# Last layer's expert rows: from indirect DMAs to products with one-hot matrices

## The reference

```
cap = EC_CAPACITY * n // N_EXPERTS                      # 2 * 512 / 16 = 64 rows per expert
affinity = softmax(h @ router_w + router_b)             # h: (512, 1024)
gates, idx = top_k(affinity.T, cap)                     # 16 experts, each picks its 64 tokens
xg = h[idx]                                             # 64 rows for each expert
hid = silu(xg @ w_gate) * (xg @ w_up)                   # weights 1024 x 1024
y = (hid @ w_down) * gates
out = zeros((512, 1024)).at[idx].add(y)                 # a token may be chosen by several experts
```

## Time and profile before

| | us |
|---|---|
| median of 3 runs (lowest, highest) | 2129.21 (2127.64, 2328.96) |
| the profiled execution's own time | 2131.61 |
| its span, first to last instruction | 2129.7 |
| PE busy | 1938.7 (91%) |
| DVE busy | 634.7 (30%) |
| ACT busy | 504.4 (24%) |
| POOL busy | 215.2 (10%) |
| mean granted TensorE clock | 0.966 of full speed |

### The profile page before, as it was taken

The page is one execution under the profiler, slowest core; times in us unless marked ns, Lnnn a source line. Parts: engine busy times, 40 slices in busy tenths (PEclk is TensorE's granted clock), DMA queues, the critical chain, the costliest instruction groups (busy, mean ns, idle before and its releaser), DMA issues. The chain is left out here.

```text
span 2129.7 us, 25643 instructions
## 1 busy us (share of the span) xinstructions
PE 1938.7 (91%) x10794; PEld 952.4 (45%) x10794; DVE 634.7 (30%) x1198; ACT 504.4 (24%) x999; POOL 215.2 (10%) x235
## 2 busy tenths in 40 slices
PE   5998999989999999999998989999898988778777
PEld 2656465544433333333334856655445323323222
DVE  2357552372431111111114366523523000000002
ACT  4145541542200000000004155514321000000002
POOL 1400000120011121211101000001101100000010
PEclk9999999999999999999998999999999998988998
DMA  9620304121389999999999123024419999999997
GB/s 348 181 79 4 136 1 165 73 79 40 113 337 399 396 394 401 393 399 396 393 389 357 45 80 139 1 81 157 158 68 403 398 401 405 401 401 405 401 401 301
DMA packets 168003, 538.73 MB, mean 253 GB/s; under 512 B 11273, under 2 KB 19795, under 8 KB 167891
## 3 DMA queue, kind: packets, MB, share of 16 engines
q1 hardware_dynamic: 149232, 489.49, 58.9%
q0 software_dynamic: 17856, 45.46, 7.2%
q10 hardware_dynamic: 802, 2.16, 0.3%
HBM read 510.08 MB, written 27.00 MB: 252 GB/s over the span
## 5 line engine op out<-in xcount | busy, mean ns | idle before, releaser
L2982 PE MATMUL ps<-ring,arena 128*64 128x512 f32 x1024 | 238.2, 616 | 25.1 <-DMA ring<-in_w_up 10.3
L2982 PE MATMUL ps<-arena 128*64 128x512 f32 x768 | 190.8, 646 | 33.2 <-DMA arena<-in_w_up 16.4
L2269 PE MATMUL ps<-arena,ring 128*128 128x256 f32 (+1 forms) x640 | 191.4, 460 | 2.4 <-DMA ring<-in_w_in 2.4
L2982 PEld LDWEIGHTS ps<-ring,arena 128*64 128x64 f32 x1024 | 76.3, 141 | 173.8 <-issue 172.5
L2269 PEld LDWEIGHTS ps<-arena,ring 128*128 128x128 f32 x640 | 120.9, 190 | 73.5 <-issue 61.1
L2175 DVE TENSOR_TENSOR arena<-arena,ps 128x512 f32<-128x512 f32 x32 | 22.0, 688 | 425.9 <-ACT arena L1414 425.9
L2822 PE MATMUL ps<-ring,arena 128*128 128x512 f32 x320 | 144.0, 605 | 0.6 <-ACT arena L1369 0.6
L2982 PEld LDWEIGHTS ps<-arena 128*64 128x64 f32 x768 | 61.8, 148 | 151.5 <-issue 151.5
L1414 ACT ACTIVATE arena<-ps 128x512 f32<-128x512 f32 x32 | 19.1, 597 | 447.6 <-PE ps L2982 447.6
L3019 PE MATMUL ps<-arena 128*64 128x512 f32 x488 | 109.7, 594 | 1.4 <-ACT arena L1437 1.4
L3019 PE MATMUL ps<-ring,arena 128*64 128x512 f32 x448 | 101.5, 595 | 3.1 <-DMA ring<-in_w_down 3.1
(11 more groups left out here) (382 smaller groups left out, 2572.7 us busy)
## 6 DMA issues: line engine op xcount, KB each, us to landing
ring<-in_w_gate SPq DMA_DIRECT2D x32, 2048.0 KB, 20.9
ring<-in_w_up SPq DMA_DIRECT2D x32, 2048.0 KB, 15.9
ring<-in_w_down SPq DMA_DIRECT2D x28, 2048.0 KB, 22.8
ring<-in_ada_w SPq DMA_DIRECT2D x24, 2048.0 KB, 11.1
arena<-in_w_down SPq DMA_DIRECT2D x22, 2048.0 KB, 23.1
arena<-in_w_gate SPq DMA_DIRECT2D x17, 2048.0 KB, 23.4
arena<-in_w_up SPq DMA_DIRECT2D x17, 2048.0 KB, 21.1
ring<-in_w_in SPq DMA_DIRECT2D x6, 2048.0 KB, 13.2
```

The costliest lines, as they stand in the source:

```text
L2269: ins = mm(o[0:n, c0:c1], w[:, k, col:col + n], hT[:, k, c0:c1], start=k == 0, stop=k == KD - 1)
L2982: ins = mm(px[0][hf * 64:hf * 64 + 64, col:col + 512], xl[e % 2][:, at:at + CAP_L], w[c][:, hf * 512:hf * 512 + 512], start=b + c == 0, st ...
```

## The change

Only the last layer changes. The homes "a" and "c" are dropped, so weights have nine homes, and "d" (the eleventh before) is the ninth. `htok` stays in SBUF, and `Fa` holds the sums there. The rows are no longer stored, gathered, added in HBM or loaded back. POOL issues nothing for the experts but one load of the table `last_no` (it tells for each column which token it is), early in the layer.

In their place, for each expert x:

- `picks(x)` (DVE, two instructions of 64 partitions by 256) compares `last_no` with the expert's row numbers and gives a one-hot matrix; `picks_turned(x)` (PE) turns it with two transposes, `picks_out(x)` (ACT) copies it from PSUM.
- `rows_up(x)` (PE) makes 8 products of the turned picks with `htok`, `picked_out(x)` (ACT) copies the rows from PSUM, and `latent_rows_turned` goes on from there.
- `spots(e)` (DVE, four instructions of 128 by 128) gives four one-hot matrices, one for each tile of 128 tokens.
- `sums_up(e, p0, p1)` (PE) makes the pieces p0 to p1 of eight, one for each tile and half of the columns. A piece is one product with 64 rows. The pieces take two PSUM banks in turn, and a piece waits until the piece two before it has been taken out.
- `sums_added(e)` (DVE) takes each piece out: for expert 0 with a copy, for the others with an addition to `Fa`, 128 by 512.

```diff
-LAST_HOMES = [0, 1, "dead", "wide", 2, 3, "b", "x", "c", "a", "d"]
+LAST_HOMES = [0, 1, "dead", "wide", 2, 3, "b", "x", "d"]
...
ACT:
                 for e in range(NE):
+                    more = not ctx_on and e + 2 < NE
                     if not ctx_on and e == NE - 1:
                         weighted(e - 1)
+                    if more and e:
+                        picks_out(e + 2)
                     hidden(e)
+                    if more:
+                        if e == 0:
+                            picks_out(2)
+                        picked_out(e + 2)
...
DVE:
+                def picks(x):
+                    dve.wait_ge(s_no, 16)
+                    if x:
+                        dve.wait_ge(S["picks_turned"], x)
+                    for h in range(2):
+                        r = slice(h * CAP_L, (h + 1) * CAP_L)
+                        ins = dve.tensor_scalar(pick[r, :], last_no[r, h * 256:(h + 1) * 256], last_rows[r, x:x + 1], None,
+                                                ALU.is_equal)
+                    ins.then_inc(S["picks_ready"], 1)
...
+                def sums_added(e):
+                    for n in range(2 * (NT - CT) * e, 2 * (NT - CT) * (e + 1)):
+                        src, _, t, hf = sum_piece(px, n)
+                        dst = Fa[:, CT + t, hf * 512:(hf + 1) * 512]
+                        dve.wait_ge(S["sums_full"], n + 1)
+                        if e:
+                            dve.wait_ge(S["sums_out"], n + 1 - 2 * (NT - CT))
+                            TT(dst, dst, src, ALU.add).then_inc(S["sums_out"], 1)
+                        else:
+                            dve.tensor_copy(dst, src).then_inc(S["sums_out"], 1)
...
                     if not ctx_on and e == NE - 1:
+                        sums_added(NE - 3)
+                        spots(NE - 1)
+                        sums_added(NE - 2)
...
+                    if not ctx_on and 2 <= e < NE - 1:
+                        sums_added(e - 2)
+                        spots(e)
                     if e + 2 < NE:
                         modulated_lat(e + 2)
                         if ctx_on:
                             modulated_ctx(e + 2)
+                        elif e + 3 < NE:
+                            picks(e + 3)
...
PE:
+                def picks_turned(x):
+                    pe.wait_ge(S["picks_ready"], x + 1)
+                    if x:
+                        pe.wait_ge(S["rows_out"], x)
+                    for c in range(2):
+                        ins = pe.transpose(px[3][:, 512 + c * P:512 + (c + 1) * P], pick[:, c * P:(c + 1) * P], ident)
+                    ins.then_inc(S["picks_turned"], 1)
+                def rows_up(x):
+                    pe.wait_ge(S["picks_out"], x + 1)
+                    for t in range(NT - CT):
+                        h, c = divmod(t, 2)
+                        for hf in range(2):
+                            ins = mm(px[3][hf * CAP_L:(hf + 1) * CAP_L, 512:1024],
+                                     pick_turned[:, c * P + h * CAP_L:c * P + (h + 1) * CAP_L],
+                                     htok[:, t, hf * 512:(hf + 1) * 512], start=t == 0, stop=t == NT - CT - 1)
+                    ins.then_inc(S["rows_up"], 1)
+                def sums_up(e, p0, p1):
+                    if p0 == 0:
+                        pe.wait_ge(S["y_lat"], n0 + e + 1)
+                        pe.wait_ge(S["spots_ready"], e + 1)
+                    for n in range(2 * (NT - CT) * e + p0, 2 * (NT - CT) * e + p1):
+                        o, i, t, hf = sum_piece(px, n)
+                        half = slice(hf * CAP_L, (hf + 1) * CAP_L)
+                        if n >= 2:
+                            pe.wait_ge(S["sums_out"], n - 1)
+                        mm(o, spot_tiles[i % 2][t][half, :], y_l[i % 2][half, :], start=True, stop=True)\
+                            .then_inc(S["sums_full"], 1)
...
                     ins = lat(0, gate, 0)
                     if e == 0:
                         ins.then_inc(S["gate_used"], 1)
+                        if not ctx_on:
+                            rows_up(1)
...
                     ins.then_inc(S["blocks_used"], 1)
+                    if not ctx_on and e == NE - 1:
+                        sums_up(NE - 2, 0, 8)
...
                 def down(e, n):
+                    sums = not ctx_on and 1 <= e < NE - 2
+                    if sums:
+                        sums_up(e - 1, 0, 3)
...
                     ins.then_inc(S["blocks_used"], 1)
+                    if sums:
+                        sums_up(e - 1, 3, 6)
...
                     latent_down(1, w).then_inc(S["down_lat"], 1)
+                    if sums:
+                        sums_up(e - 1, 6, 8)
...
-                busy_meanwhile(6 if ctx_on else 16)
+                if ctx_on:
+                    busy_meanwhile(6)
+                else:
+                    picks_turned(0)
+                    busy_meanwhile(4)
+                    rows_up(0)
+                    busy_meanwhile(4)
...
                 for e in range(NE):
+                    more = not ctx_on and e + 2 < NE
+                    if not ctx_on and e == NE - 1:
+                        sums_up(NE - 3, 0, 8)
+                    if more and e:
+                        picks_turned(e + 2)
                     gate_up(e, BLOCKS[l].index((0, e, 0)))
+                    if more and e:
+                        rows_up(e + 2)
+                    elif more:
+                        picks_turned(2)
...
                     hidden_turned(e)
+                    if more and e == 0:
+                        rows_up(2)
```

More of the change, by code:

```diff
@@ L392, in block_homes @@
         return [n % XRING[l] for n in range(6 * NE)]
-    return [LAST_HOMES[n % XRING[l]] for n in range(6 * NE - 1)] + ["d"]
+    return [LAST_HOMES[n % XRING[l]] for n in range(6 * NE)]
 def earlier_blocks(l, n):
@@ L640, in build @@
         rows_hbm = nc.dram_tensor("normed_rows", (TOK, D), F32).ap()
-        sum_hbm = [nc.dram_tensor(f"expert_sums{l}", (TOK, D), F32).ap() for l in range(DEPTH)]
+        sum_hbm = [nc.dram_tensor(f"expert_sums{l}", (TOK, D), F32).ap() for l in range(DEPTH - 1)]
         x_hbm = nc.dram_tensor("residual", (TOK, D), F32).ap()
@@ L890, in _ @@
                     pool.wait_ge(s_zero, 4)
-                    for l1 in range(DEPTH):
+                    for l1 in range(DEPTH - 1):
                         for t in query_tiles(l1):
@@ L935, in _ @@
                     pool.dma_start(Xt(t), src).then_inc(x_back[t], 16)
+                if l == DEPTH - 1:
+                    load(last_no, T["const"][:, K_END:K_END + SEQ], s_no)
                 for i, t in enumerate(q):
@@ L1419, in weighted, with picks_out, picked_out @@
                     if e >= 2:
-                        act.wait_ge(put_lat, 16 * (n0 + e - 1))
+                        act.wait_ge(*((put_lat, 16 * (n0 + e - 1)) if ctx_on else (S["sums_full"], 2 * (NT - CT) * (e - 1))))
                     act.activation(y_l[e % 2], px[1][:, 512:1024], ACT.Copy, scale=row_gate[:, e:e + 1]).then_inc(S["y_lat"], 1)
[L1423 to L1426, removed]
+                def picks_out(x):
+                    act.wait_ge(S["picks_turned"], x + 1)
+                    if x:
+                        act.wait_ge(S["rows_up"], x)
+                    act.activation(pick_turned, px[3][:, 512:768], ACT.Copy).then_inc(S["picks_out"], 1)
+                def picked_out(x):
+                    act.wait_ge(S["rows_up"], x + 1)
+                    if x:
+                        act.wait_ge(S["lat_turned"], n0 + x)
+                    act.activation(picked, px[3][:, 512:1024], ACT.Copy).then_inc(S["rows_out"], 1)
+                if not ctx_on:
+                    for x in range(2):
+                        picks_out(x)
+                        picked_out(x)
                 for e in range(NE):
+                    more = not ctx_on and e + 2 < NE
                     if not ctx_on and e == NE - 1:
                         weighted(e - 1)
+                    if more and e:
+                        picks_out(e + 2)
                     hidden(e)
+                    if more:
+                        if e == 0:
+                            picks_out(2)
+                        picked_out(e + 2)
                     if e == NE - 1:
@@ L2130, in _ @@
                 dve.wait_ge(*v.next(dve_step))
-                if not ctx_on:
-                    dve.tensor_copy(last_row, rows[:, 2 * NE - 1:2 * NE])
-                dve.tensor_copy(row_no[:, 0:NE], rows[:, NE:2 * NE])
+                if ctx_on:
+                    dve.tensor_copy(row_no[:, 0:NE], rows[:, NE:2 * NE])
+                else:
+                    dve.tensor_copy(last_rows, rows[:, NE:2 * NE]).then_inc(dve_step, 1)
+                    dve.wait_ge(*v.next(dve_step))
                 phase()
@@ L2155, in _ @@
                     modulated_ctx(1)
+                if not ctx_on:
+                    picks(0)
```

(12 more changed lines are left out.)

75 lines of the change are left out of this document (40 added, 35 removed).

## The result

The changed kernel takes 2231.96 us (median of 4 runs, 2227.15 to 2234.04). It is slower by 4.8%: the ratio to the kernel before is 1.0477, 95% interval 1.0456 to 1.0499. The forecast was 2211 us, 3.8% slower. The profiled execution took 2232.13 us, its span is 2230.3. One run of the kernel before, the 2328.96 us in the table, was in a slow state of the chip, and the ratio leaves it out.

A forecast was written before the change was run, and what follows sets the result against it. DMA was taken to bound the kernel before (32.7 us an expert), PE after (35.9). The start to 1690.6, experts 2 to 15 to 2181.6 and an end of 29.4 give a span of 2211.0; forecast 2211 us, range 2148 to 2240.

The forecast's parts named there:

- PE becomes the bound: Last layer's experts: PE needs 35.9 us for each, above the 30.7 that DMA needs, so PE sets the pace.
- The wait for the picks: Ahead of gate-and-up PE waits 3.0 us for DVE's picks (bounds 1.9 and 3.8), 2.2 in experts 0 and 1.
- The clock: Behind each picks wait gate-and-up starts at a low clock: 1.7 us more (bounds 0 and 3.4).
- The sums: Eight sum pieces for each expert on PE, in bursts of three, three and two: 5.7 us.
- The start: First products at 1631, table load behind gate_up(0), gate_up(1) at 1661.2, gate_up(2) at 1690.6 us.
- Rival A: PE keeps up and DMA stays the bound, an expert under 30.7 us: 2111 us, 0.8% faster; chance 0.12.
- Rival B: PE is the bound, but the picks wait is hidden and the clock stays up: 31.2 us an expert, 2149; chance 0.08.
- Rival C: Short gaps in the sum bursts, three per expert, keep the clock low for much of down: 2263 us; chance 0.06.

The follow-up runs named there:

- e6: The changed kernel with one home fewer ("d" dropped, eight left): 2230.46 us, ratio 1.0465.
- e1: The changed kernel with DVE making picks(e+3) right behind the hidden rows of expert e, ahead of taking out the sums: 2171.16 us, ratio 1.0200.
- e2: The changed kernel with six filler products on PE in front of each picks_turned: 2215.54 us, ratio 1.0409.
- e3: The changed kernel with the eight sum pieces as four pairs in place of three, three and two: 2211.57 us, ratio 1.0371.
- e4: The changed kernel with both the earlier picks and the sums in pairs: 2134.92 us, ratio 1.0032.
- e7: e4 with the sums of experts 12, 13 and 14 all in pairs in the last two experts: 2131.73 us, ratio 1.0001.
- e11: e7 with an earlier diagonal, last sum pair moved into the last up products, fewer fillers around rows_up(0), seven more ahead of the picks: 2125.45 us, ratio 0.9984.

## Why the prediction was right, and where it was off

- **PE becomes the bound.** Right, in mechanism and path. DMA falls to 336 GB/s in the eleven experts (about 350 forecast), the waits for weights are gone, and e6 shows that homes don't matter.
- **The wait for the picks.** Forecast 3.0 us for each expert and 2.2 twice at first; measured 3.08 and 2.13. DVE's list was as counted: its two picks take 0.71 us in place of 0.55, the spots 0.8. e1 shows that it was on the path in full.
- **The clock.** Forecast 1.7 us behind each wait, measured 1.65 by e2. e3 shows that it isn't a constant: 4.80 to 6.16 us for the same 16 records behind the same wait.
- **The sums.** This is the term that was mis-sized. I put a burst of three at 2.3 us, within bounds of 1.6 and 2.6; it measured 2.95, above the upper one. Two things were wrong. I let the first piece end 0.8 us into the burst, but DVE begins with it only 1.16 us behind the burst's start (1895.93 against 1894.77), as late as it does behind the lone third piece (1897.83 against 1896.67). And I gave the third piece 0.7 us, but alone it takes 1.05, as long as a pair. Both together are 0.65 us for a burst, 1.3 for an expert. Down beside them took 7.2 us for 6.9, rows_up 3.5 for 3.4: 16 records take 3.43 us from start to start between groups of their own shape, and 3.53 to 3.59 next to one of another shape. So 37.65 in place of 35.9. From gate_up(2) to gate_up(13), eleven experts, this made 19.6 us, in experts 13 and 14 another 1.4, and in expert 15 1.7, where a burst of eight took 7.4 us and not 6.6.
- **The start.** gate_up(2) began 3.3 us earlier than forecast. I had kept the table load of 1.28 us behind gate_up(0). It ran at 1638.1, right behind ACT's copy of the picked rows, and was out of the way; why it ran ahead there and not before isn't shown. rows_up(2) took 3.65 us for 4.5, the first gate product came 0.6 earlier, and expert 1 took 0.4 less. (The terms that the prediction gives from gate_up(0) to gate_up(1) add up to 1660.6 and not to its 1661.2.)
- **The sum of these:** 2211.0 - 3.3 + 19.6 + 1.4 + 1.7 = 2230.4, the span is 2230.3. That the start was put too late hid a part of what the sums were put too low; this much was luck. The measured 2232 lies near the upper end of the range, 2240.
- **Rival A** (DMA stays the bound, 2111 us) needed an expert in under 30.7 us. e4 shows that this could be had with another order. It then comes to 2135, not to 2111. Part of the difference is PE work outside the steady loop, the last experts' sums and the first rows: e7 to e11 took 10 us out of it. The rest no run takes apart.
- **Rival B** (no picks wait, clock up) didn't come true in the changed kernel, but e1 is what it describes. Its 31.2 us came out as 32.7, by the same mis-sized sums and neighbours.
- **Rival C** (the short gaps between pieces pull the clock down). An expert has two such gaps, one in each burst of three, and not the three that the prediction counts. In the bursts of two and three the clock didn't fall: e1 has all these gaps and a clock of 1.00 in its windows. In the bursts of eight at the end it did in 5 of 14. I had set the rival aside by an idle stretch of 1.48 us between dense products; these bursts suggest that such a stretch says little on groups of 64-row products, but no run tests that by itself. The Trainium skill, "TensorE: Matmul & The Clock Gate", section "A second HAM failure mode: psum-queue depth-cycling", tells of a kernel in which small idle gaps between groups of products that cycle through PSUM banks let the clock swing. The traces here agree in part: in e2's second burst of eight the clock fell to 0.76 (2170 to 2184 us) with only such gaps in it, while the same gaps left the changed kernel's clock at 1.00 (2172 to 2201 us).

The Trainium skill, "TensorEngine Tiling (Array Packing)", section "PSUM Bottleneck", says that tiling makes the products faster and not the emptying of PSUM. The trace agrees: two pieces on the two row halves take 1.06 us, the two additions that empty their banks 1.28.

## What to carry to other kernels

When a small result is made for a later turn of a loop (here the picks, for the expert three turns ahead), put the instruction where its inputs are ready, not where its user's neighbours stand: two instructions at the end of DVE's turn cost 4.95 us in each expert. Products through a pair of banks should come in pairs with other work between; a third one waits and then runs alone. And moving work from the bound resource to one with room pays only by what the room leaves after the waits: 10.9 us of slack for each expert would have held the 8.4 us of new products, but not 7.5 us of waits, lone pieces and lost clock on top.

## What the runs showed of the hardware that I had not expected

- A product on 64 of the rows that runs alone takes as long as two that run on both halves: 1.05 against 1.06 us for one or two products of 512 columns in float32.
- The clock fell within a burst of eight 64-row products with waits of 0.77 and 0.18 us (e2: granted 0.76 over 14 us), in 5 of 14 such bursts, while the other nine with the same waits kept it. Waits of 0.78 us with 3.6 us and more of dense products between them left it at 1.00 in e1's eleven experts.
- Behind the same wait of 3.08 us the following 16 records took 4.80, 5.24 or 6.16 us. An edit that shortens something else can change this share: e3 lost about 0.4 us for each expert in this way.
